# Low parts of Q and K subtracted on VectorE instead of GpSimd, in a two-layer streaming encoder on one core

## The reference

```python
h = rms(x, g_mix_pre)
q1, q2, k1, k2, v, ux, ug, ga, gb = split(h @ w_in)      # 8 heads, head_dim 64, v_dim 128
s1 = q1 @ k1.T * scale + bias; s2 = q2 @ k2.T * scale + bias   # ALiBi, chunk mask
o = (softmax(s1) - lam * softmax(s2)) @ v                # per head, then rms over the head
branch_a = o @ w_branch_attn
branch_b = (rg_lru(conv(ux)) * gelu(ug)) @ w_branch_lru  # width-4 conv, gated recurrence
m = sigmoid(ga) * branch_a + sigmoid(gb) * branch_b
x = x + rms(m @ w_out, g_mix_post)
x = x + rms(square(relu(rms(x, g_mlp_pre) @ w_up)) @ w_down, g_mlp_post)
```

## Time and profile before

| | |
|---|---|
| three runs | 2031.54, 2032.9 and 2036.31 us, median 2032.9 |
| the profiled execution's own time | 2029.05 us |
| its span, first to last instruction | 2027.2 us |
| TensorE busy | 1985.7 us, 98% |
| VectorE, ScalarE, GpSimd busy | 1069.3 (53%), 955.3 (47%), 277.9 us (14%) |
| mean granted TensorE clock | 0.993 |
| the 32 subtractions on GpSimd (L628) | 45.2 us in all, 1364 ns the median one |

### The profile page before, as it was taken

One profiled execution on the slowest core, in us unless ns is written; L12 is line 12 of the kernel. 1 busy time (PEld: TensorE's weight loads), 2 busy tenths in 40 slices (PEclk: granted clock), 3 DMA queues, 4 the chain that ended last, 5 costly groups with the idle time before them and its releaser, 6 DMA issues.

```text
span 2027.2 us, 38778 instructions
## 1 busy us (share of the span) xinstructions
PE 1985.7 (98%) x15694; PEld 1939.5 (96%) x15694; DVE 1069.3 (53%) x1976; ACT 955.3 (47%) x1503; POOL 277.9 (14%) x302
## 2 busy tenths in 40 slices
PE   7999999999999999999999999999999999999997
PEld 7999999999999999999989999999999999999997
DVE  6657576765437432343456676757645474224334
ACT  5466656565236431332365756565732554213323
POOL 4212111100101200120041212020001012002100
PEclk9999999999999999999999999999999999999998
DMA  5323232222332232333313232322223323233322
GB/s 137 108 68 93 69 93 69 83 69 80 91 95 72 83 92 85 89 88 90 98 53 99 73 97 72 89 73 78 74 84 89 99 64 92 84 93 84 93 84 67
DMA packets 308455, 172.00 MB, mean 85 GB/s; under 512 B 7592, under 2 KB 303872, under 8 KB 308320
## 3 DMA queue, kind: packets, MB, share of 16 engines
q1 hardware_dynamic: 300768, 155.47, 26.8%
q0 software_dynamic: 7520, 14.59, 2.6%
q10 hardware_dynamic: 32, 0.04, 0.0%
HBM read 158.86 MB, written 11.21 MB: 84 GB/s over the span
## 4 chain that ended last, share of the span: by engine, by line
PE 81%; ACT 9%; DVE 6%; issue 2%; DMA 0%; SPq 0%; ACTq 0%; DVEq 0%
PE PJ L687 65%; PE PJ L699 4%; PE PJ L859 4%; PE PX L887 2%; ACT w_hi L1115 2%; DVE w_lo L1590 1%; PE PX L905 1%; PE PX L925 1%; DVE T L1701 1%; PE PX L941 1%; PE PX L699 1%; DVE uc L1831 1%; ACT L1332 1%; DVE Y L1622 1%; ACT L1145 1%
## 5 line engine op out<-in xcount | busy, mean ns | idle before, releaser
L1590 DVE TENSOR_TENSOR w_lo<-w_raw,w_hi 128x1024 fp32r<-128x1024 f32 x284 | 384.5, 1359 | 370.3 <-ACT w_hi L1115 369.6
L687 PE MATMUL PJ<-h_hi,w_hi 128*128 128x272 f32 x2304 | 490.7, 294 | 2.6 <-DVE T L1701 1.9
L687 PE MATMUL PJ<-h_hi,w_lo 128*128 128x272 f32 x2304 | 475.6, 289 | 0.0
L687 PE MATMUL PJ<-h_lo,w_hi 128*128 128x272 f32 x2304 | 474.6, 288 | 0.0
L1115 ACT ACTIVATE w_hi<-w_raw 128x1024 fp32r<-128x1024 f32 x284 | 297.8, 1051 | 234.0 <-DMA w_raw<-in_w_down 116.4
L687 PEld LDWEIGHTS PJ<-h_hi,w_hi 128*128 128x128 f32 x2304 | 360.2, 189 | 12.8 <-issue 9.5
L687 PEld LDWEIGHTS PJ<-h_lo,w_hi 128*128 128x128 f32 x2304 | 361.5, 189 | 0.0
L687 PEld LDWEIGHTS PJ<-h_hi,w_lo 128*128 128x128 f32 x2304 | 360.3, 189 | 0.0
L687 PE MATMUL PJ<-u_hi,w_hi 128*128 128x272 f32 x960 | 198.4, 288 | 0.0
L687 PE MATMUL PJ<-u_hi,w_lo 128*128 128x272 f32 x960 | 197.4, 288 | 0.0
L687 PE MATMUL PJ<-u_lo,w_hi 128*128 128x272 f32 x960 | 197.1, 287 | 0.0
(11 more groups left out here) (341 smaller groups left out, 3511.4 us busy)
## 6 DMA issues: line engine op xcount, KB each, us to landing
w_raw<-in_w_in SPq DMA_DIRECT2D x110, 512.0 KB, 3.8
w_raw<-in_w_down SPq DMA_DIRECT2D x64, 512.0 KB, 3.8
w_raw<-in_w_up SPq DMA_DIRECT2D x62, 512.0 KB, 4.2
w_raw<-in_w_branch_attn SPq DMA_DIRECT2D x16, 512.0 KB, 3.8
w_raw<-in_w_branch_lru SPq DMA_DIRECT2D x16, 512.0 KB, 3.8
w_raw<-in_w_out SPq DMA_DIRECT2D x16, 512.0 KB, 3.7
out_prompt_k<-stage POOLq DMA_DIRECT2D x16, 256.0 KB, 2.8
out_prompt_v<-GA POOLq DMA_DIRECT2D x8, 512.0 KB, 4.0
```

What stands on the lines that cost most here:

```text
L687: mm = pe.matmul(PJ[:, buf, half, 0:HT], w[a], src[b][:, k0 + k, HT * half:HT * half + HT], start=first and k == 0 and a + b == 0, stop=en ...
L1590: dve.tensor_tensor(low(n)[:], raw(n), w_hi[:, n.hi, :, :].bitcast(F32), ALU.subtract).then_inc(w_lo_ready, 1)
```

## The change

The subtraction that makes `qk_lo` moves from GpSimd's stream to VectorE's, in a function `qk_rest`. VectorE runs it for tile i - 1 directly ahead of the eviction of tile i (for tile 3 in step 4, behind that step's `split_lo`); for p = 0 tiles 0 and 1 come together ahead of `qk_tile(2)`. It waits for ScalarE's `qk_hi_ready` of its tile. GpSimd keeps `store_k` for both K tiles, one behind the other.

```diff
@@ gpsimd
-                    for i in range(4):
-
-                        pool.wait_ge(qk_hi_ready, 4 * g + i + 1)
-                        pool.tensor_tensor(qk_lo[:, i, :], T[:, i % 2, :], qk_hi[:, i, :].bitcast(F32), ALU.subtract).then_inc(qk_lo_ready, 1)
-                        if i >= 2:
-                            store_k(l, p, i - 2)
+                    for m in range(2):
+                        store_k(l, p, m)
@@ vector
+            def qk_rest(l, p, i):
+
+                dve.wait_ge(qk_hi_ready, 4 * (4 * l + p) + i + 1)
+                dve.tensor_tensor(qk_lo[:, i, :], T[:, i % 2, :], qk_hi[:, i, :].bitcast(F32), ALU.subtract).then_inc(qk_lo_ready, 1)
+
@@ vector, order of a pair
                         if i == 2 and p == 0:
                             split_lo(pair_tile(l, p, 5))
+                        if p == 0 and i == 2:
+                            qk_rest(l, p, 0)
+                        if p > 0 and i > 0 or i > 1:
+                            qk_rest(l, p, i - 1)
                         if p > 0 and i < 4 or i in (2, 3):
                             qk_tile(l, p, i)
```

## The result

The changed kernel takes 2036.75 us, the kernel before 2032.85 (medians of 20 runs each, 2031.93 to 2042.46 and 2029.97 to 2036.9). The ratio is 1.0015, 95% interval 1.0009 to 1.0021, so 1.8 to 4.3 us more, and 3.0 in the middle; the two medians lie 3.9 us apart. In a second series the ratio was 1.0020, 1.0011 to 1.0029 (12 and 29 runs). Forecast were +2.3 us and 2035.2. The profiled execution took 2033.82 us, with a span of 2032.0.

What follows compares the result with a forecast made beforehand. TensorE, busy 98%, bounds the kernel, waiting in six pairs for a tanh behind VectorE's fourth eviction. Six times 0.65 - 0.30 = 0.35 is 2.1 us, plus 0.2 for p = 0: +2.3, so 2035.2 us, range 2030 to 2039.5.

Steps and rivals of the forecast that it cites:

- The chain that sets the wait: In six pairs (p = 1 to 3), VectorE's `qk_tile(3)` sets ScalarE's tanh and TensorE's K transposes; delay passes one to one.
- Tile 2's rest costs 0.65, all on the path: Ahead of tile 3's eviction on VectorE, with no idle time there: 0.65 us per pair, p = 1 to 3.
- The splits give back 0.30: Two VectorE weight splits before the convolution, freed of GpSimd's overlapping subtraction: 0.30 us earlier per pair, bounds 0 and 0.47.
- Tiles 0, 1 and 3 cost nothing: For p = 1 to 3, their rests fit VectorE idle time of 0.66, 1.20 and 0.78 us: value 0 each.
- p = 0: First pair of each layer: TensorE newly waits 0.2 us for `rs_tok` in layer 1, 0 in layer 0; bounds 0 and 0.6.
- GpSimd's stores are not touched: GpSimd's queue only gets shorter; K stores still start when ScalarE's staging lets them: value 0.
- The sum: Whole kernel: 2.1 us from six pairs plus 0.2 for the first pairs, +2.3 us, giving 2035.2 us.
- rival 4: TensorE's clock falls, 1.4 us each: one may vanish (+0.9, 2033.8) or one or two come (+3.7 to +5.1); chance 0.13.
- Rival 1: Each rest costs more than 0.65 in VectorE's queue through its waits; with 0.84, +5.1 us, 2038.0; chance 0.13.
- rival 2: VectorE's two weight splits keep 2.68 us whatever GpSimd does: +4.3 us, 2037.2; chance 0.09.
- Rival 3: First weight split stands still for all 0.47 us of GpSimd overlap and regains it: +1.3 us, 2034.2; chance 0.12.
- No change that can be measured: Whole kernel: 0.11% more, under the about 0.2% (4.1 us) a measurement can tell; chance of within 0.72.

## Why the prediction was right

- *The chain that sets the wait* (VectorE's fourth eviction, ScalarE's tanh, TensorE's transposes): right. One more instruction of 0.64 there is 0.64 more wait, taking the instruction away removes the wait, and twice tile 3's rest does nothing.
- *Tile 2's rest costs 0.65, all on the path*: 0.63.
- *The splits give back 0.30*: 0.32. The net is 0.30 to 0.31 per pair, where 0.35 was forecast. The prediction called the split at 1045.70 undisturbed; a GpSimd subtraction lay over its first 0.15 us and cost it nothing:

```profile
1044.49 1.36 POOL L628 TENSOR_TENSOR qk_lo<-T,qk_hi 128x544 fp32r<-128x544 f32 x1 [3.75 <-ACT qk_hi L1235]
```

- *Tiles 0, 1 and 3 cost nothing*: right for tiles 0 and 3, which were tried one by one; tile 1's rest was tried only together with them, and T behind it was idle for 0.57 in the changed kernel. Tile 0's is free only just: with it twice T was 0.52 late and the wait 0.54 longer. Its 0.08 of cover was real: T starts 1.89 behind the split in the kernel before and in the one with tile 2 on GpSimd alike.
- *p = 0*: 0 in layer 0, right. In layer 1 the term of 0.2 was 0.78 in the profile, most of it through a late DMA, and in six later profiles 0.28, 0.22 and four times nothing that is listed. The chain of VectorE that it was worked out from was right (5.42 for 5.50 us).
- *GpSimd's stores are not touched*: right; `store_k` waits for ScalarE as before.
- *The sum*, +2.3: by the waits 1.4 + 0.8 = 2.2 in the profile, and that this comes so near is partly luck. The prediction said 3.9 us of waits for the tanh and 3.2 came: 0.3 of the difference is the net per pair, 0.4 the one long wait of the kernel before, which was taken for a lasting one; and the 0.8 is a late DMA. Without both chances it is 6 x 0.31 = 1.9 and 0 to 0.3 for `rs_tok`. The runs gave 3.0, interval 1.8 to 4.3, and 4.1, interval 2.2 to 5.9. The clock would account for 0.3 to 1.1 us of that (rival 4); the forecast's own sum left it out.
- *Rival 1* (an instruction with its waits costs 0.84) is refuted by 0.63 and 0.64, *rival 2* (no relief) by 2.36 and by the kernel with one subtraction beside the splits, where 2.68 came back.
- *Rival 3*, which is the rule of the Trainium skill's "SBUF — State Buffer", "Who interferes with whom", was refuted in its number and borne out in its mechanism. By the profile's times, overlaps of 0.15, 0.47 and 1.29 us cost VectorE nothing, 0.30 to 0.32 and 1.09. It is 0.15 to 0.2 short of the overlap each time, not a share of it. So blocked for the whole instruction fits, if the instruction frees VectorE 0.15 to 0.2 us before its end in the profile; that reading is an inference from these overlaps. The choice of 0.30 was right because it was measured.
- *"No change that can be measured"*: the ratios, 1.0015 and 1.0020, are within or at 0.2%, but with 20 runs the interval shuts zero out. The bound of 0.2% was too cautious for a series of that length.

The version to keep is the one that leaves each rest to VectorE but behind the eviction: 2028.1 to 2028.7 us, 0.22 to 0.24% under the kernel before and some 0.4% under the changed one. With only tile 2's rest moved there it is 2028.6, which the runs can't tell from it. The eviction is what ScalarE and TensorE wait for; nobody asks for the low part until the scores.

## What to carry to other kernels

When an instruction moves to an engine that is half idle, its cost is not its length but what stands behind it in that queue at that place: 24 of 32 moves were free here within what the runs can tell, apart from what they add in front of `rs_tok`, and of the other eight the six with p > 0 carried the added wait for the tanh. Put work that nobody waits for behind the instruction that somebody waits for, even if the diff reads more naturally the other way round. And follow each wait of the bounding engine back through the queues before a move; here waits of 0.24 us were enough to name the one place that mattered.

## What was not expected of the hardware

- VectorE and GpSimd took turns by whole instructions: beside three GpSimd subtractions VectorE's two splits took 3.85 us instead of 2.36 and GpSimd's three 6.0 instead of 4.1, while an overlap of 0.15 us cost nothing.
- A fall of TensorE's clock at a pair's start gives the other engines cover. With tile 0's rest twice the wait was 1.09 where the clock held and 0.52 where it fell, so a profile with a fall at the wrong place hides what it is meant to show.
- The mean granted clock differs between kernels in which TensorE does the same work: 0.9919 to 0.9921 before, and 0.9931 to 0.9933 with the rests on VectorE behind the evictions.
